# Encoder trunk on one core: norm vectors loaded as rows and transposed, bias writes on SyncE's queue, x copied by VectorE alone, and the second product's weights fetched ahead of the spill

## What is computed

```python
h = concat([meta_tokens, x])                     # (1040, 1024)
u = h * rsqrt(mean(h*h, -1) + 1e-6) * norm_mix[0]
q, k, v = split(u @ a_w_qkv)                     # 16 heads of 64
for each grid row r:                             # a window of 8 rows and 16 columns around each query
    s = q @ k_window.T + a_rel_bias[head, dr, dc]    # outside the window: -inf
    s_meta = q @ k_meta.T + a_meta_bias
    o = softmax([s, s_meta]) @ [v_window, v_meta]
h = h + o @ a_w_o
h = h + (silu(n @ w1) * (n @ w3)) @ w2           # n = rmsnorm(h, norm_ffn[0])
...                                              # layer 2: norm_mix[1], grouped attention, norm_ffn[1]
return rmsnorm(h, norm_final)[meta:]
```

## Time and profile before

| | |
|---|---|
| time, median of 3 runs | 3090.8 us |
| the profiled execution's own time | 3092.26 us |
| its span | 3090.5 us |
| mean granted TensorE clock | 0.966 |
| TensorE matmul busy | 2853.5 us (92%) |
| VectorE / ScalarE / GpSimd busy | 42% / 21% / 43% of the span |
| DMA | 167.68 MB, 54 GB/s over the span |

### The profile page before, as it was taken

One profiled execution on the slowest core, in us unless ns is written; L12 is line 12 of the kernel. 1 busy time (PEld: TensorE's weight loads), 2 busy tenths in 40 slices (PEclk: granted clock), 3 DMA queues, 4 the chain that ended last, 5 costly groups with the idle time before them and its releaser, 6 DMA issues.

```text
span 3090.5 us, 40619 instructions
## 1 busy us (share of the span) xinstructions
PE 2853.5 (92%) x15386; PEld 2358.5 (76%) x15386; DVE 1289.7 (42%) x1621; ACT 655.7 (21%) x1126; POOL 1342.0 (43%) x1389
## 2 busy tenths in 40 slices
PE   4899999699999999999997599999699999999994
PEld 4788888499999999999886344444478888888883
DVE  2244444434223232225656566665352322223335
ACT  3243343411000000002100355554210000000001
POOL 1556555344444444444321266554254444444440
PEclk8899999899999999999999699999899999999996
DMA  6222121311111111112221100000311111111111
GB/s 171 49 61 60 51 54 44 132 48 45 44 44 45 47 49 48 45 48 93 63 68 49 56 1 35 36 1 14 145 44 43 53 48 48 46 44 46 50 44 59
DMA packets 233411, 167.68 MB, mean 54 GB/s; under 512 B 30880, under 2 KB 215840, under 8 KB 232624
## 3 DMA queue, kind: packets, MB, share of 16 engines
q1 hardware_dynamic: 212208, 123.03, 14.1%
q10 hardware_dynamic: 21056, 42.57, 3.9%
HBM read 136.69 MB, written 29.32 MB: 54 GB/s over the span
## 4 chain that ended last, share of the span: by engine, by line
PE 81%; DVE 9%; issue 3%; DMA 2%; ACT 1%; ACTq 1%; SPq 1%; POOL 0%; DVEq 0%; POOLq 0%
PE PS L602 58%; PE PS L715 8%; PE PS L921 3%; DVE nmx L1581 2%; PE PS L933 2%; PE PS L758 2%; PE PS L794 2%; PE PS L734 2%; DVE rcp L1624 2%; PE PS L879 1%; SPq L370 1%; DMA oraw<-o_spill 1%; PE PS L854 1%; PE PS L631 1%; DMA bias_rows<-vt 1%
## 5 line engine op out<-in xcount | busy, mean ns | idle before, releaser
L429 POOL TENSOR_TENSOR wh<-wraw,ones 128x512 fp32r<-128x512 f32 (+1 forms) x456 | 412.5, 905 | 1307.6 <-PE PS L602 1117.7
L602 PE MATMUL PS<-uh,wh 128*128 128x348 f32 (+1 forms) x2120 | 528.3, 349 | 23.6 <-POOL wl L432 10.2
L432 POOL TENSOR_TENSOR wl<-wraw,wh 128x512 fp32r<-128x512 f32 (+1 forms) x456 | 514.1, 1127 | 35.8
L602 PE MATMUL PS<-ul,wh 128*128 128x348 f32 (+1 forms) x2120 | 523.3, 346 | 0.0
L602 PE MATMUL PS<-uh,wl 128*128 128x348 f32 (+1 forms) x2120 | 522.5, 346 | 0.0
L602 PEld LDWEIGHTS PS<-uh,wh 128*128 128x128 f32 x2120 | 371.4, 189 | 61.2 <-issue 22.2
L602 PEld LDWEIGHTS PS<-ul,wh 128*128 128x128 f32 x2120 | 373.6, 189 | 31.9
L602 PEld LDWEIGHTS PS<-uh,wl 128*128 128x128 f32 x2120 | 371.7, 188 | 30.4
L1355 DVE TENSOR_TENSOR h<-PS,h 128x1044 f32<-128x1044 f32 (+1 forms) x192 | 236.9, 1234 | 334.3 <-PE PS L602 334.3
L1019 ACT ACTIVATE at<-at 128x1044 f32<-128x1044 f32 (+1 forms) x44 | 47.1, 1070 | 864.6 <-DVE at L1367 864.6
L602 PE MATMUL PS<-gh,wh 128*128 128x348 f32 (+1 forms) x880 | 223.3, 351 | 1.6 <-DVE h L1355 1.6
(11 more groups left out here) (187 smaller groups left out, 3766.2 us busy)
## 6 DMA issues: line engine op xcount, KB each, us to landing
wraw<-in_ffn_w SPq DMA_DIRECT2D x176, 256.0 KB, 2.9
wraw<-in_ffn_w SPq DMA_DIRECT2D x176, 128.0 KB, 2.2
wraw<-in_a_w_qkv SPq DMA_DIRECT2D x48, 256.0 KB, 2.8
biasb<-bias_rows SPq DMA_DIRECT2D x256, 36.0 KB, 1.9
oraw<-o_spill ACTq DMA_DIRECT2D x16, 522.0 KB, 6.6
h<-h_spill ACTq DMA_DIRECT2D x16, 522.0 KB, 10.5
qkv_spill<-tq ACTq DMA_DIRECT2D x12, 522.0 KB, 2.7
h_spill<-h SPq DMA_DIRECT2D x8, 522.0 KB, 6.8
```

Source lines behind the costliest of these rows:

```text
L429: nc.gpsimd.tensor_tensor(wh[:, slot, 0:w], wraw[:, slot, 0:w], ones[:, 0:1].to_broadcast([P, w]), ALU.mult).then_inc(s_whi, 1)
L432: nc.gpsimd.tensor_tensor(wl[:, slot, 0:w], wraw[:, slot, 0:w], wh[:, slot, 0:w].bitcast(F32), ALU.subtract).then_inc(s_wrd, 1)
L602: mm = nc.tensor.matmul(PS[:, set_ + c, 0:cw], w, x[k][:, c * cw:(c + 1) * cw], start=(first and i == 0 and ti == 0), stop=(last and i == ...
```

## The change

Five parts, all in the first hundred microseconds:

1. The norm vectors are loaded as rows, `graw` (40, 128): five transfers of 8 rows of 512 bytes. TensorE transposes `graw` into PSUM bank 0 ahead of the x tiles, and VectorE copies the result to `gains`.
2. The zero fill of `bias_rows` is issued on ScalarE's queue right behind them, ahead of all activations.
3. The 16 bias writes move from ScalarE's queue to SyncE's, behind weight units 0 and 1, with a wait for the fill.
4. x tiles go into PSUM bank pairs (6, 7) and (4, 5) in turn; VectorE alone copies both banks of a tile in one instruction of 128 x 1024. ScalarE only squares.
5. On SyncE's queue units 2 and 3 go ahead of the spill, and the bias tables of pair 1 (`load_bias(1)`) go behind units 4 to 7.

```diff
             fetch_chunk(0, w_qkv, 0)
+            sp.wait_ge(s_bfill, 16)
+            for c in range(CB):
+                sp.dma_start(bias_rows[:, c, 4:19, c + 1:c + 32], A["a_rel_bias"][0], ...).then_inc(s_brow, 16)
+            fetch_chunk(2, w_qkv, D)
             sp.wait_ge(s_pad, 3)
             sp.wait_ge(s_xra, 9)
-            sp.wait_ge(s_xrb, 9)
             for m in range(KC):
                 sp.dma_start(h_spill[:, m, :], h[:, m, :]).then_inc(s_hsp, 16)
-            fetch_chunk(2, w_qkv, D)
             load_bias(0)
-            load_bias(1)
             fetch_chunk(4, w_qkv, 2 * D)
             fetch_chunk(6, w_qkv, P)
+            load_bias(1)
...
+            pe.wait_ge(s_graw, 80)
+            nc.tensor.transpose(PS[:, 0, 0:5 * KC], graw[:, :], ident[0:5 * KC, 0:5 * KC]).then_inc(s_gt, 1)
             for i in range(9):
                 pe.wait_ge(s_xl[i], 16)
+                if i >= 2:
+                    pe.wait_ge(s_xra, i - 1)
+                for k in range(KC):
+                    mm = nc.tensor.transpose(PS[:, X_BANK[i % 2] + k // 4, k % 4 * n:(k % 4 + 1) * n],
+                                             xt[0:n, i, k * P:(k + 1) * P], ident[0:n, 0:n])
+                mm.then_inc(s_xt, 1)
...
-            act.dma_start(gains[:, 0, :], A["norm_mix"][0].rearrange("(k p) -> p k", p=P), ...
+            for i, gain in enumerate((A["norm_mix"][0], A["norm_ffn"][0], A["norm_mix"][1], A["norm_ffn"][1],
+                                      A["norm_final"])):
+                act.dma_start(graw[KC * i:KC * i + KC, :], gain.rearrange("(k p) -> k p", p=P)).then_inc(s_graw, 16)
+            act.wait_ge(s_zero, 1)
+            act.dma_start(bias_rows..., vt...).then_inc(s_bfill, 16)
...
+            dve.wait_ge(s_gt, 1)
+            nc.vector.tensor_copy(gains[:, :, :].rearrange("p g k -> p (g k)"), PS[:, 0, 0:5 * KC]).then_inc(s_const, 1)
             for i in range(9):
-                nc.vector.tensor_copy(h[:, 0:4, P * i:P * i + n], PS[:, 6, 0:4 * n]...).then_inc(s_xra, 1)
+                nc.vector.tensor_copy(h[:, :, P * i:P * i + n]..., PS[:, X_BANK[i % 2]:X_BANK[i % 2] + 2, 0:4 * n]...
+                                      ).then_inc(s_xra, 1)
```

More of the change, by code:

```diff
@@ L58 @@
 PV_AT = [2, 5, 7, 8]
+X_BANK = [6, 4]
 HID = 2816
@@ L136, in build @@
         gains = sb("gains", [P, 5, KC], F32)
+        graw = sb("graw", [5 * KC, P], F32)
         ssx = sb("ssx", [P, 9], F32)
@@ L205, in build @@
         s_id = sem("ident_loaded")
-        s_const = sem("gains_loaded")
+        s_graw = sem("gain_rows_loaded")
+        s_gt = sem("gains_transposed")
+        s_const = sem("gains_ready")
         s_raw = [sem("raw_slot0_loaded"), sem("raw_slot1_loaded")]
@@ L693, in _ @@
                 pe.wait_ge(s_xl[i], 16)
[L694 to L701, removed]
+                if i >= 2:
[4 more added lines that the diff above has]
+                mm.then_inc(s_xt, 1)
+            pe.wait_ge(s_const, 1)
+            pe.wait_ge(s_xra, 9)
             pe.wait_ge(s_pad, 3)
@@ L1078, in _ @@
                                      accum_out=ssx[0:n, i:i + 1]).then_inc(s_xsq, 1)
-                if i == 0:
-                    act.wait_ge(s_zero, 1)
-                    act.dma_start(bias_rows.rearrange("h c a e -> (h c a e)").rearrange("(p n) -> p n", p=P),
-                                  vt[:, :, :].rearrange("p a b -> p (a b)")[:, 0:NH * CB * ARR * EW // P]
-                                  ).then_inc(s_bfill, 16)
-                if i == 3:
-                    act.wait_ge(s_bfill, 16)
-                if 3 <= i <= 6:
-                    for c in range(4 * (i - 3), 4 * (i - 2)):
-                        rel_bias(c)
-            act.wait_ge(s_const, 80)
+            act.wait_ge(s_const, 1)
             act.wait_ge(s_xra, 9)
-            act.wait_ge(s_xrb, 9)
             def u_hi(m):
@@ L1416, in _ @@
             nc.vector.memset(ssx[:, :], 1.0).then_inc(s_pad, 1)
+            dve.wait_ge(s_gt, 1)
+            nc.vector.tensor_copy(gains[:, :, :].rearrange("p g k -> p (g k)"), PS[:, 0, 0:5 * KC]).then_inc(s_const, 1)
             for i in range(9):
                 n = P if i < 8 else META
-                dve.wait_ge(s_xt, 2 * i + 1)
-                nc.vector.tensor_copy(h[:, 0:4, P * i:P * i + n],
-                                      PS[:, 6, 0:4 * n].rearrange("p (c n) -> p c n", n=n)).then_inc(s_xra, 1)
+                dve.wait_ge(s_xt, i + 1)
+                nc.vector.tensor_copy(h[:, :, P * i:P * i + n].rearrange("p (b c) n -> p b c n", b=2),
+                                      PS[:, X_BANK[i % 2]:X_BANK[i % 2] + 2, 0:4 * n]
+                                      .rearrange("p b (c n) -> p b c n", n=n)).then_inc(s_xra, 1)
             dve.wait_ge(s_xsq, 9)
             nc.vector.tensor_scalar(ssv[:, :], ssx[:, :], 1.0 / D, EPS, ALU.mult, ALU.add).then_inc(s_rv, 1)
-            dve.wait_ge(s_const, 80)
+            dve.wait_ge(s_const, 1)
             dve.wait_ge(s_pad, 3)
```

26 lines of the change are left out of this document (6 added, 20 removed).

## The result

The change makes the kernel faster, by about half of what was forecast: 3071.98 us, median of 5 runs (3066.55 to 3073.06), against 3090.8 (3088.64 to 3098.75) on the same chip, a ratio of 0.9928 with a 95% interval of 0.9908 to 0.9947. That is 19 us by the medians and 22 by the ratio; forecast were 43, to 3048 (3041 to 3062). The profiled execution took 3072.74, its span is 3070.2 (3090.5 before), the granted clock 0.971.

The account below looks back on a forecast made before the run. TensorE bounds the kernel, so only its idle time at the start counts: v starting at 57.8 instead of 100.43 (42.6) plus 0.7 for warmer matmuls makes 43.3 of 3092.26; on the medians' scale 3048 us, range 3041 to 3062.

Parts of the forecast that it names:

- The frame: Whole kernel: TensorE is 81% of the chain, so gains come only where it idles, here by v's earlier start.
- What it gains at the start is passed on whole: Behind the start: nothing later waits for a fixed time, so the whole gain reaches the end.
- x is all there at about 16: Start of the kernel: without 4-byte norm packets, x loads at 413 GB/s and is whole at about 16 us.
- 36 (no faster than before): Upper bound for the end of x's load, against 16 taken and 13.5 as the lower bound.
- rival B: x loads no faster, as something other than 4-byte packets slows the start; `uh` at 37.7, total 3064 us; chance 0.09.
- as soon as they thin out: Argument against x loading no faster: 363 GB/s once the 4-byte packets thin out.
- Part 1's second effect: Zero fill on ScalarE's queue: issued near 4.5 us and landed at 11, where it had landed at 40.2.
- Part 4: x tiles: 1.83 us of transposes each, VectorE's 1.23 copy overlapping; `uh` starts at 21.2 instead of 53.62.
- Parts 3 and 5: SyncE's queue: bias writes 10.5 us, spill landed at 37.8, v's weights split by 52.5, idle 10.19 ahead of v closed.
- Rival A: Zero fill lands at 24.5 instead of 11, holding SyncE's queue; gain 33, total 3058 us; chance 0.14.
- C: SyncE's queue serves the 16 bias writes one by one, 78 us; slower, total 3113 us; chance 0.03.
- The sign that I named for C: In the profile after: bias writes with landings beyond 10 us would speak for one-by-one service.

Follow-up runs that it names:

- a_consec: The kernel after with each x tile loaded from 128 consecutive tokens instead of 8 groups of 16 rows (another result): 3059.62 us, ratio 0.9882 to the kernel before.
- b_consec: The kernel before with each x tile loaded from 128 consecutive tokens, norm vectors still in 4-byte pieces (another result): 3074.51 us, ratio 0.9935 to the kernel before.
- a_oldgains: The kernel after with part 1 undone, norm vectors again as 4-byte elements and the fill behind them on ScalarE's queue: 3079.97 us, ratio 0.9949 to the kernel before.
- a_act7: The kernel after with part 4 undone, x tiles in banks 6 and 7 only, ScalarE copying one and VectorE the other: 3071.97 us, ratio 0.9913.
- a_same: The kernel after, unchanged, run again on another occasion: 3070.39 us, ratio 0.9925 to the kernel before.
- a_bothload: The kernel after with `load_bias(1)` put back ahead of units 4 to 7: 3077.59 us, ratio 0.9936 to the kernel before.
- a_scatter: The kernel after with x tiles of 128 rows lying 32 KB apart in DRAM, 128 outermost (another result): 3056.23 us, a single execution.
- a_wide: The kernel after, same result, with x in 16 transfers that each write 16 partitions of four tiles: 3074.60 us, ratio 0.9933 to the kernel before.
- a_dst16: The kernel after with x in transfers onto 16 partitions of four tiles, each read from one contiguous 256 KB run (another result): 3078.95 us, a single execution.
- a_strip32: The kernel after with x in eight transfers of eight groups, each writing 32 partitions of four tiles (another token order): 3062.77 us, a single execution.
- a_strip64: The kernel after with x in eight transfers of eight groups, each writing 64 partitions of two tiles (another token order): 3075.34 us, a single execution.

## Why the prediction was wrong

**The frame held for this pair of executions, in part by luck.** The kernel gained what v's earlier start and its faster clock gained, 18.4 of 20.3 us. "What it gains at the start is passed on whole" is too strong, though, as a_consec beside the kernel after shows: v starts 20.5 earlier, but the span is only 11.9 shorter. At the first load of `oraw`, behind layer 1's attention, 17.4 of it still stand (560.97 and 543.56), at the first `fin`, at the end, 12.5 (3033.68 and 3021.20). What goes with it is the granted clock: a_consec's is 0.51 from 515 to 518.4 us and 0.50 from 1437 to 1440 and from 1471 to 1474, the kernel after's is 1.00 from 72 to 555 and from 592 to 1650. (1.00 is the upper of its two levels, 2.4 GHz, and 0.50 the lower, 1.2 GHz.) From v's start to the end the 20 profiled executions need 2985.7 to 2994.3 us, and the kernel after's is the shortest, by 2.8. So its profile flatters it, and behind v's start executions differ by up to 9 us; this is part of why a_consec's time fell by less than expected.

**The step that failed is part 1's: "x is all there at about 16", "since packets of the same size ran at 413".** The cause that I put down, 4-byte packets in the way, was wrong (b_consec). The upper bound in the text, "36 (no faster than before)", is what came: x was not all there at 16, and the last tile's transposes start at 37.91, when its data is in. What held x was its transfers' eight groups at the source: half of the engines, share 0.52, 130 to 134 GB/s, where the forecast had 413. With x in 128 groups, and nothing else changed, `uh` starts at 21.64 (a_consec). I had the row that speaks for it: 145 GB/s at a share of 0.60, of which the 4-byte packets held 5.5% and x's queue 59.1%. The 4-byte packets of b_consec stand beside a share of 98.4% and don't bring it down, so a share of 0.60 called for another cause, and rival B (0.09) deserved the greater chance. And the 363 GB/s "as soon as they thin out" was not x set free. The queues of the kernel before from 33 to 35 us, which the forecast left out:

```profile
q10 hardware_dynamic: 187, 0.42, 56.4%
q1 hardware_dynamic: 139, 0.30, 47.1%
```

SyncE's queue moved 0.30 MB in those 2 us, 150 GB/s, as before; the rest is the fill.

**Rival B's sum, 3064, was still 8 too small.** Its `uh` at 37.7 came at 41.44 (3.7). Its bias writes, "issued from 24 to 34.6", took from 24.56 to 44.86, because a ring full of x issues at x's pace; so the spill, issued at 46.16, landed at 64.65 where B had 56.6. q then stood 8.78 on VectorE, and k's matmuls, issued after a gap, took 14.20. B's scores end at 74.3, the real ones at 84.51.

**Part 1's second effect was right and it is the one that pays.** The fill, issued at 3.12, was landed by 13 (forecast 11), and without part 1 the kernel is 6 to 7 us slower (a_oldgains).

**Part 4**: 1.23 for the copy held, and a tile took 1.97 (1.83 forecast), but nothing of it counts where x is late (a_act7). In a_consec, where x is not, `uh` starts at 21.64, and that the forecast said 21.2 is luck, for two errors cancel. The transposes started at 8.99, not 6.2, and the last five tiles took not 1.83 but 1.06 or 1.07 each:

```profile
8.99 4.91 PE L704 MATMUL PS<-ident,xt 128*128 128x128 f32 x24
14.07 1.06 PE L704 MATMUL PS<-ident,xt 128*128 128x128 f32 x8 [0.17 <-DVE h L1406]
```

The prediction took the faster weight loads at 37.37 as a sign that transposes had raised the clock. The profile gives the granted clock as 1.00 at 35.41 and at 37.37 alike, so the row doesn't tell. What the runs add: a_consec's tiles had only transposes ahead of them and went from 1.64 each to 1.06, and in a_same a tile took 1.09 at a granted clock of 1.00 (25.65) and 1.97 at 0.50 (28.05). But the kernel after's 1.97 stand at 1.00 as well, so whether it is the clock stays open.

In a_consec the rest of the sum can be checked too. v starts at 64.01 (forecast 57.8), and the terms that were too small are the bias writes in a busy ring (13.13, not 10.5), the spill (17.4 from first issue to landed, not 14.4), which q waits for 7.95, and the cold k behind it (13.89). Of the 42.6 by which v was to start earlier, 15.9 came, the shape of x took 20.5 (84.51 - 64.01) and these terms 6.2. In a_same, at the faster rate of eight engines, v starts at 75.52 and the shape takes 11.5.

**Parts 3 and 5** were right in kind: the idle stretch ahead of v closed, and v ran in 11.65 (13.20 in a_consec) instead of 14.12 (forecast 13.4); with the 32 loads put back it opens again (a_bothload). The load behind units 4 to 7, 14.90 at 83.71, cost nothing. Rival A (fill late) and C (bias writes one by one) didn't come. The sign that I named for C, a landing beyond 10 us, did: the first bias write needs 10.9 in the kernel after, but behind x and not one by one, so it was no sign of C.

## What to carry to other kernels

Look at the DMA share before the rate: where a share stopped at one half here with only large transfers in flight, the reason was in the transfer's outermost dimension, eight, and not in what shared the queue. The loads that ran at 395 GB/s and more had 16 or 128 groups at the outside of the source and wrote all 128 partitions. Put nothing on a queue between data and a spill that the next stage waits for without counting the full ring: an issue that costs 0.6 us in an empty one took up to 8.17 here. And before you trust that a gain at the start is passed on whole, compare a late landmark in both traces.

## What the runs showed of the hardware

- Eight groups at the source: a share of 0.50 to 0.52, as of eight engines, on either queue, at 130 to 200 GB/s from one execution to another. 128 rows, near or 32 KB apart: a share of 1.02 to 1.03 at 418 and 420 GB/s (a_consec and a_scatter, 12 to 16 us).
- 16 engines that write strips of 16 partitions are all busy and move 121 to 125 GB/s (a_wide from 16 to 36 us, a_dst16 from 16 to 32).
- Eight engines that write four partitions each, none 32 apart: 209 to 217 GB/s (a_strip32, 16 to 24 us); in pairs 32 partitions apart: 125 to 141 (a_strip64, 16 to 32 us).
- 425 packets of 4 bytes between 425 of SyncE's queue, mostly of 4 KB: 6.4% of the engines' time.
- The transposes of one tile took 1.97 with waits between tiles; right behind 24 others they took 1.06 (a_strip32 at 22.74, a_consec at 14.07).
